# Gathering the first expert pair in fp32, turning the second pair's rows inside the first down product, and sharing the last result rows out over three engines

## What is computed

```python
h = layer_norm(DEEPNORM_ALPHA * h + mix, ln_mix_g[l], ln_mix_b[l])
ffn = grouped_moe(h, w_router, router_bias, w_gate[l], w_up[l], w_down[l])
h = layer_norm(DEEPNORM_ALPHA * h + ffn, ln_ffn_g[l], ln_ffn_b[l])
...
for e in range(N_EXPERTS):
    y = (jax.nn.silu(hf @ w_gate[e]) * (hf @ w_up[e])) @ w_down[e]
    out = out + gates[:, e:e + 1] * y
```

## Time and profile before

| | before |
|---|---|
| median of 3 runs | 641.98 us (641.68 to 643.27) |
| the profiled execution | 642.98 us, its span 640.9 us |
| PE busy | 618.2 us, 96% |
| DVE, ACT, POOL busy | 47%, 33%, 23% |
| mean rate of all transfers | 385 GB/s, 246.72 MB |

### The profile page before, as it was taken

One profiled execution on the slowest core, in us unless ns is written; L12 is line 12 of the kernel. 1 busy time (PEld: TensorE's weight loads), 2 busy tenths in 40 slices (PEclk: granted clock), 3 DMA queues, 4 the chain that ended last, 5 costly groups with the idle time before them and its releaser, 6 DMA issues.

```text
span 640.9 us, 8180 instructions
## 1 busy us (share of the span) xinstructions
PE 618.2 (96%) x3239; PEld 333.0 (52%) x3239; DVE 304.0 (47%) x623; ACT 211.2 (33%) x469; POOL 148.5 (23%) x139
## 2 busy tenths in 40 slices
PE   8999999999999999997999999999999999999893
PEld 5887886434344344342488878763344344344231
DVE  6899897222142141130578988871042141231226
ACT  5832964232032032030194268352032032031111
POOL 1999300620000000000049971007000000000000
PEclk9999999999999999999999999999999999999997
DMA  8999399899999999999998646989999999999991
GB/s 357 432 424 399 129 423 415 316 431 429 427 424 426 427 424 429 425 425 427 431 428 360 235 197 275 419 333 398 431 422 430 425 427 426 428 425 427 430 389 70
DMA packets 21498, 246.72 MB, mean 385 GB/s; under 512 B 3244, under 2 KB 3372, under 8 KB 6352
## 3 DMA queue, kind: packets, MB, share of 16 engines
q1 hardware_dynamic: 17712, 234.46, 87.2%
q10 hardware_dynamic: 1728, 7.87, 3.1%
q0 software_dynamic: 2016, 3.82, 1.6%
HBM read 246.51 MB, written 3.15 MB: 390 GB/s over the span
## 4 chain that ended last, share of the span: by engine, by line
PE 79%; DMA 12%; DVE 7%; issue 1%; ACT 1%; DVEq 0%
PE bank L747 28%; PE bank L770 15%; PE bank L639 13%; DMA ring<-in_units 11%; PE bank L796 4%; PE bank L613 4%; PE bank L852 2%; DVE w_split L1459 2%; PE bank L864 2%; PE bank L718 2%; PE bank L684 1%; PE bank L627 1%; PE bank L757 1%; PE bank L934 1%; PE bank L567 1%
## 5 line engine op out<-in xcount | busy, mean ns | idle before, releaser
L747 PE MATMUL bank<-ring,xe_pair 128*64 128x512 f32 x992 | 217.3, 593 | 7.9 <-DMA ring<-in_units 7.9
L747 PEld LDWEIGHTS bank<-ring,xe_pair 128*64 128x64 f32 x992 | 70.3, 137 | 151.0 <-issue 134.8
L1688 DVE TENSOR_TENSOR area_b<-area_b,bank 128x512 f32<-128x512 f32 x16 | 11.0, 687 | 207.2 <-PE bank L747 207.2
L770 PE MATMUL bank<-ring,area_b 128*64 128x512 f32 x480 | 107.0, 596 | 1.6 <-DVE area_b L1690 1.6
L1315 POOL DMA_INDIRECT rows<-normal_rows,tiny_i x14 | 14.4, 1026 | 265.3 <-DVE tiny_i L1638 242.4
L1299 POOL TENSOR_TENSOR in_lo<-ring,in_hi 128x512 fp32r<-128x512 f32 x56 | 71.7, 1327 | 12.3 <-ACT in_hi L1062 12.3
L1145 ACT ACTIVATE area_b<-bank 128x512 f32<-128x512 f32 x16 | 9.6, 597 | 185.7 <-PE bank L747 185.7
L770 PEld LDWEIGHTS bank<-ring,area_b 128*64 128x64 f32 x480 | 32.8, 137 | 66.9 <-issue 59.0
L1123 ACT ACTIVATE xe_pair<-bank,small 128x128 f32<-128x128 f32 x128 | 46.3, 468 | 45.0 <-PE bank L718 35.6
L1266 POOL TENSOR_TENSOR rstd<-var_eps,tiny 128x1 f32<-128x1 f32 x18 | 10.6, 593 | 194.6 <-DVE var_eps L1391 194.6
L1709 DVE SCALAR_TENSOR_TENSOR y_lo<-bank,tiny,y_hi 128x512 fp32r<-128x512 f32 x32 | 24.0, 751 | 59.7 <-ACT y_hi L1158 59.7
(11 more groups left out here) (208 smaller groups left out, 794.3 us busy)
## 6 DMA issues: line engine op xcount, KB each, us to landing
ring<-in_units SPq DMA_DIRECT2D x105, 2048.0 KB, 20.3
ln_par<-in_ln_rows ACTq DMA_DIRECT2D x4, 1024.0 KB, 11.4
extra<-in_units SPq DMA_DIRECT2D x4, 1024.0 KB, 7.8
extra<-in_units SPq DMA_DIRECT2D x2, 1536.0 KB, 20.1
ring<-in_units SPq DMA_DIRECT2D x2, 1024.0 KB, 8.1
normal_rows<-mix ACTq DMA_DIRECT2D x4, 512.0 KB, 7.0
h<-in_x SPq DMA_DIRECT2D x2, 512.0 KB, 4.0
piece_area<-in_branch_rows ACTq DMA_DIRECT2D x2, 512.0 KB, 7.4
```

Source lines behind the costliest of these rows:

```text
L747: mm = pe.matmul(bank[2 + m][e * SLOTS:(e + 1) * SLOTS, :], x[:, k, at + e * SLOTS:at + (e + 1) * SLOTS], w[:, c, m, e, :], start=k == 0, ...
L770: mm = pe.matmul(bank[5 + n][e * SLOTS:(e + 1) * SLOTS, :], hidT[:, k, e * SLOTS:(e + 1) * SLOTS], w[:, k, e, :], start=k == 0, stop=k == ...
```

## The change

1. `first_pair` multiplies `normal` itself, in fp32, with an fp32 `first_pick`: 16 matmuls, chunk by chunk, so that the first chunks are complete early. `n_hi` and `first_lo` aren't made any more in this pass.
2. As nothing lies in the place of `extra[1]` now, SP loads it whole, without waiting for the gather.
3. `turn_rows(1)` moves from between `gate_up(0)` and the other transposes into `down(0)`, between its halves, and goes to banks 7 and 4; ACT scales these tokens after the first half of `y_hi`. `gate_up(1)` then waits chunk by chunk. POOL waits for the turned rows of a pair before it gathers those of the next but one.
4. At the end, columns 512 to 1023 of block 1 are made by ACT (centre and scale) and POOL (gain, shift). DVE makes the rest. SP waits for POOL's semaphore for the last quarter.

```diff
-        first_pick = nc.alloc_sbuf_tensor_at("first_pick", [P, TB, P], F32R, offset=area_b_at + 4096)
+        first_pick = nc.alloc_sbuf_tensor_at("first_pick", [P, TB, P], F32, offset=area_b_at + 4096)
...
-TURN_BANKS, MORE_BANKS = (5, 6), (0, 1, 7, 4)
+TURN_BANKS, MORE_BANKS = ((7, 4),) + ((5, 6),) * (PAIRS - 2), (0, 1, 7, 4)
...
                     if k == EXTRAS[1]:
-                        sp.dma_start(extra[1][:, UNIT // 2:], src[:, UNIT // 2:]).then_inc(extra_landed[1], 16)
-                        sp.wait_ge(main_sems["gathered"], CHUNK_PAIRS * (l + 1))
-                        sp.dma_start(extra[1][:, 0:UNIT // 2], src[:, 0:UNIT // 2]).then_inc(extra_landed[1], 16)
+                        sp.dma_start(extra[1][:, :], src).then_inc(extra_landed[1], 16)
...
-                sp.wait_ge(result_ready, n + 2)
+                if n == 0:
+                    sp.wait_ge(result_ready, 2)
+                else:
+                    sp.wait_ge(tail_ready, 1)
...
-                def first_pair(part):
+                def first_pair():
                     for b in range(TB):
                         wait_pick(b)
-                        pe.wait_ge(n_hi_ready if part is n_hi else n_lo_ready, TB * l + b + 1)
-                        for c in range(KC):
+                    for c in range(KC):
+                        for b in range(TB):
                             mm = pe.matmul(bank[FIRST_BANKS[c // 2]][:, c % 2 * P:(c % 2 + 1) * P],
-                                           part[:, b, c * P:(c + 1) * P], first_pick[:, b, :],
...
+                                           normal[:, b, c * P:(c + 1) * P], first_pick[:, b, :],
+                                           start=b == 0, stop=b == TB - 1)
+                        if c % 2 == 1:
+                            mm.then_inc(s["gathered"], 1)
...
-                            if j == 0 and m == 0:
-                                wait_xe(0, k + 1)
+                            if (j == 0 or ps.main and j == 1) and m == 0:
+                                wait_xe(j, k + 1)
...
-                        if ps.main and j + 1 < pairs:
+                        if ps.main and 0 < j < pairs - 1:
                             wait_xe(j + 1, 4 * (n + 1))
+                        if ps.main and j == 0 and n == 1:
+                            turn_rows(1)
...
-                    if ps.main and j + 1 < pairs:
+                    if ps.main and 0 < j < pairs - 1:
                         turn_rows(j + 1)
...
-            def normal_high(l, b):
+            def save_normal(l, b):
                 act.wait_ge(norm_ready, TB * l + b + 1)
-                act.activation(n_hi[:, b, :], normal[:, b, :], ACT.Copy).then_inc(n_hi_ready, 1)
                 act.dma_start(normal_rows[l][b * P:(b + 1) * P, :], normal[:, b, :]).then_inc(normal_saved, 16)
...
+                        if ps.main and j == 0 and n == 0:
+                            turned_tokens(1)
...
+            act.wait_ge(mean_scaled, 1)
+            act.activation(acc[:, 1, BANK:D], acc[:, 1, BANK:D], ACT.Identity, scale=rstd[:, n_ln - 1:n_ln],
+                           bias=last_shift).then_inc(tail_centred, 1)
...
-                pool.wait_ge(n_lo_ready, TB * (l + 1))
...
                     pool.wait_ge(used, l * LAYER_UNITS + SLABS + PAIR_UNITS * (j - 2) + 4)
+                    pool.wait_ge(main_sems["rows_turned"], 2 * (l * (PAIRS - 1) + j - 1))
                     rows_of_pair(l, j)
...
+            tail = h[:, 1, BANK:D]
+            pool.wait_ge(tail_centred, 1)
+            pool.wait_ge(par_in, 16 * (2 * DEPTH + 1))
+            pool.tensor_tensor(tail, tail, ln_par[:, 0, BANK:D], ALU.mult).then_inc(gain_step, 1)
+            pool.wait_ge(gain_step, products[0] + 1)
+            pool.tensor_tensor(tail, tail, ln_par[:, 1, BANK:D], ALU.add).then_inc(tail_ready, 1)
...
-            def normal_low(l, b):
-
-                dve.wait_ge(n_hi_ready, TB * l + b + 1)
-                dve.tensor_tensor(first_lo[:, b, :], normal[:, b, :], n_hi[:, b, :].bitcast(F32), ALU.subtract)\
-                   .then_inc(n_lo_ready, 1)
...
-                    norm_apply(norm[0], acc[:, 0, :], h[:, 0, :], 0, ln_par[:, 0, :], ln_par[:, 1, :], result_ready)
-                    step(dve.scalar_tensor_tensor(out=h[:, 1, :], in0=acc[:, 1, :], scalar=mv[:, 1, 0:1], in1=ln_par[:, 0, :],
+                    step(dve.scalar_tensor_tensor(out=h[:, 0, :], in0=acc[:, 0, :], scalar=mv[:, 0, 0:1], in1=ln_par[:, 0, :],
                                                   op0=ALU.subtract, op1=ALU.mult))
                     dve.wait_ge(ln_rstd, norm[1] + 1)
-                    for n in range(2):
...
+                    dve.tensor_scalar(last_shift, mv[:, 1, 0:1], rstd[:, norm[1]:norm[1] + 1], -1.0, ALU.mult, ALU.mult)\
+                       .then_inc(mean_scaled, 1)
+                    dve.scalar_tensor_tensor(out=h[:, 0, :], in0=h[:, 0, :], scalar=rstd[:, norm[0]:norm[0] + 1],
+                                             in1=ln_par[:, 1, :], op0=ALU.mult, op1=ALU.add).then_inc(result_ready, 1)
+                    norm_apply(norm[1], acc[:, 1, 0:BANK], h[:, 1, 0:BANK], 1, ln_par[:, 0, 0:BANK], ln_par[:, 1, 0:BANK],
+                               result_ready)
```

More of the change, by code:

```diff
@@ L55 @@
 EXTRAS = (RING, RING + 1)
-EXTRA_LOADS = (2, 2)
 EARLY = 3072
@@ L242, in trunk @@
         slot_gate = tiny[:, 6:8]
+        last_shift = tiny[:, 5:6]
         qk_rows = area_a[:, 0:2048].rearrange("p (b n) -> p b n", b=TB)
@@ L341, in trunk @@
         result_ready = sem("result_ready")
+        mean_scaled = sem("mean_scaled")
+        tail_centred = sem("tail_centred")
+        tail_ready = sem("tail_ready")
         ln_var = sem("ln_var")
@@ L1139, in turned_tokens @@
                         for c in range(4 * half, 4 * half + 4):
-                            scaled_tokens(xe_pair[j % 2][:, c, :], bank[TURN_BANKS[half]][:, c % 4 * P:(c % 4 + 1) * P], c)
+                            scaled_tokens(xe_pair[j % 2][:, c, :], bank[TURN_BANKS[j - 1][half]][:, c % 4 * P:(c % 4 + 1) * P], c)
                 gathered_tokens()
@@ L1238, in _ @@
                                    scale=rstd[:, i:i + 1]).then_inc(router_sig, 1)
-                normal_high(l, 0)
-                normal_high(l, 1)
+                save_normal(l, 0)
+                save_normal(l, 1)
                 main, more = passes[l]
```

23 lines of the change are left out of this document (5 added, 18 removed).

## The result

The change makes the kernel slower: **644.14 us** in the median of 8 runs (643.66 to 644.83), against 641.92 us of the kernel before on the same chip (8 runs, 641.56 to 643.27). The ratio is 1.0031, 95% interval 1.0021 to 1.0041, so 2.0 us more, 1.3 to 2.6. (The medians themselves lie 2.2 us apart; the ratio and its interval are what is used from here on.) The forecast was 639.7 us with a range of 637.5 to 641.6. Both were wrong, and so was the sign.

The account below looks back on a forecast made before the run. The prediction took each expert stage to end when its weight stream ends, with PE having some 4 us of slack. Its terms, -1.2 and -1.5 us for the layers and +0.4 for the tail, made -2.3: 639.7 us, range 637.5 to 641.6.

Parts of the forecast that it names:

- the price of the gather: First pair's gather: 16 fp32 matmuls at 0.126 us take 2.0 us, so pair 0's matmuls start 1.5 us earlier.
- The first load: First ring load of layer 0's expert stage: issued at 118.27 in place of 119.77, counting from 119.95.
- the stages' -1.2 and -1.5 us: Expert stages: the weight stream ends earlier by 1.2 us in layer 0 and 1.5 us in layer 1.
- rival C: Gather: each fp32 matmul takes four steps of 113 ns, 7.2 us in all, and the run 649.9 us; chance 0.04.
- The tail: Program end: VectorE and GpSimd take turns, with about 0.3 us of each handover overlapped; +0.4 us, bounds -0.6 and +1.1.
- The lost time of the DMA engines: Before the weight stream, 10 us from 114 and 427: 3.9 and 4.2 us lost, 2.7 us each after the change.
- rival A: Saved rows fill the gap before 119.9 and the tail has no lock: layers 2 x 2.0, tail -0.5, 637.5 us; chance 0.13.
- PE's pair 0: Expert stage, with the turn moved: pair 0 takes 0.5 us more from its start, at no cost to the run.
- late rows: Pair 1's saved rows end at worst 2.5 us later; gathered by 132.2, their turn comes at 134, covered with 2 us to spare.
- GpSimd's wait for the turned rows: Before pair 2's gather: the new wait is over at 135.1; row numbers came only after 134 before.
- Removed rounding: Two ScalarE activations and two VectorE subtractions a layer go: no gain, as they ran beside the routing and the gather.
- B: Small gain: 0.9 us off each layer and a fully serial tail of +1.1, 641.3 us; chance 0.26.

Follow-up runs that it names:

- e4: Changed kernel with the old tail, pair 0 gathered from rounded tokens alone in one pass, rest of the rounding left out: 639.97 us, 0.9960 of the kernel before.
- e2: Changed kernel with the old tail (parts 1 to 3 without part 4): 642.62 us, 1.0006 of the kernel before.
- e1: Kernel before with the new tail alone (part 4 and nothing else): 643.25 us, 1.0021 of the kernel before.
- e5: Changed kernel with VectorE's halves of block 1 taken from PSUM, GpSimd keeping both operations on columns 0 to 511: 642.34 us, 1.0003 of the kernel before.
- e7: Changed kernel with the old tail and the second extra loaded in two halves, the second behind the gather: 643.06 us, 1.0009 of the kernel before.
- e6: Changed kernel with the old tail and the turn of pair 1's rows at its old place: 643.40 us, 1.0021 of the kernel before.

## Why the prediction was wrong

**The step that failed is the price of the gather:** "I take that one, the same operation: 16 x 0.126 = 2.0 us". The operation was the right one and the row was right, 8 in 1.16 us. I divided by the row's count, and the count is of the engine's instructions. L924 stands in a loop over `GROUPS = 4`, so its 8 records are four matmuls: 1.16 us for four. The same is at L747, where `gate_up` has 32 matmuls and the row x64, and at L770, where `down` has 16 and the row x32; the text ahead of the prediction calls them 64 and 32, and it is wrong in that. The fp32 transposes do not count double: the turn has eight of them and its row x8. At 2 x 0.12 = 0.24 us a matmul the gather is 16 x 0.24 = 3.8, and 3.81 was measured. At e4's 16 records it is 1.97.

**What hung on it.** The first load was to go out at 118.27 and went out at 119.94, so the stages' -1.2 and -1.5 us could not be. e4 shows that the step behind the price was sound: with a short gather the run is 2.6 us faster. My rival C had the right kind of mechanism, an fp32 product that costs several steps. By its sum a gather of 3.2 us gains nothing, and one of 3.8 us costs 0.5 and 0.2 us in the two layers. The runs do not contradict that (e2: +0.4 us, -0.3 to 1.0), but none lies between 1.97 and 3.81 us to test the threshold. I gave it 0.04 since "the 126 ns of L924 speak against it", the same misread row. The Trainium skill (FP8 and Floating Point Precision, "TensorE Precision Notes") has true fp32 in four passes. The traces here agree with a multiple but not with four: two records for each matmul, and a gather of 3.81 us for 16, where four steps of 113 ns would have made 7.2.

**The tail: right mechanism, wrong size.** This is the second term that was off. I had taking turns, with 0.3 us of each handover overlapped, and +0.4 us; measured +1.35 in e1 (0.7 to 2.0), and 1.4 in the span. VectorE is through with block 0 at 636.42 and with its last half at 639.76, 3.34 us for which I had 2.7: the handovers overlap by 0.2 us and not by 0.3, and GpSimd's operations grow too, to 1.39 and 1.59 us from my 1.18 (1.26 where neither waits, e5). To that comes SP: its second output was to be issued 0.35 us after the first and the pair takes 0.82. Even the upper bound of +1.1 lies below the 1.4 of the span, since it ended with the last operation and left out the second output behind it; e1's interval still holds it.

**The lost time of the DMA engines.** I reckoned 3.9 us lost in 114 to 124 from 258 GB/s. The share of 0.77 in the same row says 2.3 us of idle; the rest is work on small packets (1.00 and 328 GB/s from 120 to 124 in the kernel before, where the rows of pair 1 are among it). So part of what I counted as a gap was the row gather. It filled the gap in the kernel before, and with the extra loaded whole it comes 2.3 us later, on the stream. That is the contrary of rival A. It cost nothing that shows (e7 against e2).

**PE's pair 0** was to take 0.5 us more and takes 0.93 more: from 116.32 to 140.77 (24.45 us), before from 116.14 to 139.66 (23.52). The new wait at L757 (0.4 us) was in the forecast. But taking the turn away shortens the way from the end of gate/up to the down product only from 2.56 to 2.28 us, where I had 0.5 less; and with the turn inside it the down product takes 8.26 us and not 7.08, where I had 1.0 more. That it costs nothing is not contradicted: PE still waits for the ring, and by some 0.7 us a layer less.

The **late rows** were right: they are saved 8.5 to 10.4 us after their issue, the turn is late enough, and e6 speaks for its being needed. GpSimd's wait for the turned rows was not as short as forecast: it was to be over at 135.1, and pair 2's gather goes out at 138.03, before at 135.28. PE waits for no rows even so.

**Removed rounding** at nothing was not contradicted; no run tests it alone. **B** (641.3 us, a small gain and a serial tail) was the nearest of my cases below the kernel before, and its -0.9 a layer was still too good.

**What stays open:** whether the stages of the changed kernel cost 0.4 us or nothing (e2's interval holds both, and so do the stage sums in e4; the gather is 0.2 us a layer longer), and the 0.25 us between the sum of e1 and e2 and the whole. Profiles of the same code differ by more than that: block 0's last statistics after the same layer 0 start at 318.89 in the kernel before and at 318.29 in e1. Whether a short gather with the whole computation can be had (a single pass on rounded tokens whose rest is added elsewhere) was not tried.

## What to carry to other kernels

Before a row's time is divided by its count, hold the count against the loop in the source: an fp32 matmul stands as two records here, so a mean per record is half the price of a matmul, and two rounded parts cost about as much as one fp32 product (3.60 and 3.81 us). Before work is handed from VectorE to GpSimd, see that VectorE's operations beside it have an input in PSUM; else reckon them almost one after the other (0.2 us overlapped here), and add that GpSimd's operations grow as well. Even without the waiting the hand-over gained nothing here (e5). And bytes moved forward gain nothing if what stands behind them in the queue isn't moved too: ask what will be in the gap that they leave.

## What the runs showed of the hardware

- An fp32 matmul stands as two instructions on TensorE, each with its own weight load: 16 of 128x128 by 128 in 3.81 us, 0.24 each; 32 of 64 wide by 512 columns in 13.73 us, 0.43 each. On rounded tokens (e4) 16 stand as 16, in 1.97 us. An fp32 transpose stands as one: 8 in 1.02 us.
- A VectorE operation of 128x512 with two SBUF inputs takes 0.75 us alone, and 1.75, 1.64 and 1.82 beside GpSimd operations that read SBUF; with one input in PSUM it takes 0.70 to 0.75 beside the same, whether it writes to PSUM or to SBUF. GpSimd's own takes 1.26 beside VectorE's work from PSUM, 1.59 when it has to wait.
- The normalised rows (4 KB each), written beside an extra loaded whole (2 MB), land after 8.5 to 10.4 us in the changed kernel and after up to 10.83 in e6; in the kernel before it is 6.1 to 8.9. With pair 1's rows fetched among the load (120 to 124 us in the kernel before) the DMA engines show a share of 1.00 and move 328 GB/s, where the stream alone has 426 at 1.01.
